# Attention of the first layer in 37 steps of up to four pairs of heads instead of 56 steps of one pair

## The reference

```python
def even_layer(x, mem_n, ...):
    h = rms_norm(x, norm_g)
    (nq, nkc, nvc, nks, nvs, nkw, nvw, ng, nz, mq, mk, mv, mz, eq, ez) = _split(h @ w_in, EVEN_SPLITS)
    gates = sigmoid(ng + gate_b)                       # 3 branches x 8 heads
    a_out = nsa_attention(rot(nq), kc, vc, rot(nks), nvs, rot(nkw), nvw, gates)
    b_out = moba_attention(rot(mq), rot(mk), mv)       # 8 heads of 64
    m_out = memory_attention(eq, mem_n, w_mem_kv)      # 4 heads of 64 over 256 memory rows
    y = concatenate([a_out * silu(nz), b_out * silu(mz), m_out * silu(ez)]) @ w_out
    return x + y
```

## Time and profile before

| | us |
|---|---|
| median of 3 runs | 2300.81 (2300.05 to 2301.47) |
| profiled execution | 2301.48 |
| its span, first to last instruction | 2299.7 |
| TensorE busy in the span | 2222.7 (97%) |
| DVE busy | 666.7 (29%) |
| ACT busy | 502.7 (22%) |
| mean granted clock of TensorE | 0.987 |

### The profile page before, as it was taken

The page is one execution under the profiler, slowest core; times in us unless marked ns, Lnnn a source line. Parts: engine busy times, 40 slices in busy tenths (PEclk is TensorE's granted clock), DMA queues, the critical chain, the costliest instruction groups (busy, mean ns, idle before and its releaser), DMA issues. The chain is left out here.

```text
span 2299.7 us, 19928 instructions
## 1 busy us (share of the span) xinstructions
PE 2222.7 (97%) x8070; PEld 1049.2 (46%) x8070; DVE 666.7 (29%) x1189; ACT 502.7 (22%) x996; POOL 0.2 (0%) x4
## 2 busy tenths in 40 slices
PE   9999999999999999999999999999989989999897
PEld 5444455544444444444444455554445333333333
DVE  3355545412311222411343333331140010100134
ACT  3333334310000324211123334230121000000022
POOL 0000000000000000000000000000000000000000
PEclk9899999999999999999999999999999999999998
DMA  9211112122222111123211121132346999999950
GB/s 230 57 37 37 37 37 74 47 82 74 88 92 76 46 49 54 42 81 80 74 61 50 37 74 37 38 83 73 146 165 258 405 409 409 409 409 409 409 207 37
DMA packets 164602, 317.40 MB, mean 138 GB/s; under 512 B 44800, under 2 KB 74624, under 8 KB 164512
## 3 DMA queue, kind: packets, MB, share of 16 engines
q1 hardware_dynamic: 162480, 314.41, 37.8%
q10 hardware_dynamic: 2032, 1.73, 0.3%
HBM read 314.01 MB, written 2.10 MB: 137 GB/s over the span
## 5 line engine op out<-in xcount | busy, mean ns | idle before, releaser
L417 PE MATMUL bank<-hT,ring 128*128 128x512 f32 (+1 forms) x1632 | 742.5, 605 | 6.8 <-ACT hT L579 4.8
L417 PEld LDWEIGHTS bank<-hT,ring 128*128 128x128 f32 (+1 forms) x1632 | 304.5, 192 | 366.4 <-issue 357.5
L417 PE MATMUL bank<-ring,hT 128*128 128x512 f32 (+2 forms) x576 | 219.6, 539 | 0.0
L2255 PE MATMUL bank<-wide,xg 128*64 128x512 f32 x600 | 179.1, 595 | 9.4 <-DMA wide<-in_w_exp_up 2.8
L417 PEld LDWEIGHTS bank<-ring,hT 128*128 128x128 f32 x576 | 103.1, 190 | 106.3 <-issue 102.7
L2255 PE MATMUL bank<-ring,xg 128*64 128x512 f32 x392 | 132.9, 596 | 4.7 <-DMA ring<-in_w_exp_gate 3.4
L417 PE MATMUL bank<-rz,ring 128*128 128x512 f32 x256 | 111.3, 592 | 0.0
L2255 PEld LDWEIGHTS bank<-wide,xg 128*64 128x64 f32 x600 | 54.7, 137 | 97.1 <-issue 96.1
L2290 PE MATMUL bank<-wide,hidT 128*64 128x512 f32 x304 | 89.3, 595 | 6.4 <-ACT hidT L2346 3.5
L417 PEld LDWEIGHTS bank<-rz,ring 128*128 128x128 f32 x256 | 48.6, 190 | 61.2 <-issue 61.0
L1177 ACT ACTIVATE att_pt<-bank 128x512 f32<-128x512 f32 (+3 forms) x56 | 38.6, 688 | 161.4 <-PE bank L1056 161.3
(11 more groups left out here) (433 smaller groups left out, 2218.6 us busy)
## 6 DMA issues: line engine op xcount, KB each, us to landing
wide<-in_w_exp_gate SPq DMA_DIRECT2D x76, 512.0 KB, 12.5
wide<-in_w_exp_down SPq DMA_DIRECT2D x76, 512.0 KB, 13.7
wide<-in_w_exp_up SPq DMA_DIRECT2D x74, 512.0 KB, 13.3
ring<-in_l_w_in SPq DMA_DIRECT2D x18, 2048.0 KB, 7.8
ring<-in_w_exp_gate SPq DMA_DIRECT2D x52, 512.0 KB, 12.2
ring<-in_w_exp_down SPq DMA_DIRECT2D x52, 512.0 KB, 13.2
ring<-in_w_exp_up SPq DMA_DIRECT2D x46, 512.0 KB, 13.5
ring<-in_w_in SPq DMA_DIRECT2D x10, 2048.0 KB, 7.7
```

What stands on the lines that cost most here:

```text
L417: mm = pe.matmul(self.out(n), *mats[i], start=i == 0, stop=i == len(mats) - 1)
L2255: mm = pe.matmul(bank[2 * which + n][e * 64:(e + 1) * 64, :], xg[p // 2 % 2][:, k, s:s + CAP], block_ap(j)[k % 2][:, n * 512:(n + 1) * 512 ...
```

## The change

The units are made of one, two or four pairs, so that their scores fill 512 columns of a bank: query tile t takes `4 // (t + 1)` pairs at once (four of 128 keys, two of 256, one of 384 or 512), the memory two of 256. NSA's query tiles come in the order 3, 2, 1, 0. That makes 22 units of NSA (8, 8, 4, 2), 11 of MoBA (1, 2, 4, 4) and 4 of memory: 37. The instructions of DVE on a unit span its pairs; the exponentials are still one per head and pair. The dense jobs are cut into four quarters, of two products each (112 in all), and laid evenly over the 37 steps: three in each, four in the last. The four jobs of mz and their block of weights come before those of mv. Silu and the gating of groups move to the steps that follow from this; the small statistics' tile `att_stats` is placed in the arena.

```diff
-            ("mq", 1816, 512), ("mk", 2328, 512), ("mv", 2840, 512), ("mz", 3352, 512)]:
+            ("mq", 1816, 512), ("mk", 2328, 512), ("mz", 3352, 512), ("mv", 2840, 512)]:
...
+        def several(t):
+            n = 4 // (t + 1)
+            return [range(i, i + n) for i in range(0, 4, n)]
+
+        for t in reversed(range(TT)):
+            groups.append(dict(first=len(units), y=proj[:, NZ:NZ + 4, t * P:(t + 1) * P], tile=t))
+            for branch, tile in ((1, NKS), (2, NKW)):
+                keys = [proj[e * 64:(e + 1) * 64, tile, 0:(t + 1) * P] for e in range(2)]
+                share = gates[:, t, 8 * branch:8 * branch + 8].rearrange("p (g i) -> p g i", g=2)
+                for some in several(t):
+                    add_unit([(heads_of(NQ + i, t), keys) for i in some], t + 1,
...
-        def planned(n, parts=2):
-            nonlocal slot_at
+        def planned(n, parts=4):
             step = 8 // parts
             for i in range(parts):
-                plan[slot_at].append((n, i * step, (i + 1) * step))
-                slot_at += 1
+                quarters.append([(n, i * step, (i + 1) * step)])
 
         def planned_turns():
             n = len(jobs)
             flush()
-            for x in range(n, len(jobs)):
-                plan[slot_at - 1].append((x, 0, 8))
+            quarters[-1].extend((x, 0, 8) for x in range(n, len(jobs)))
...
+        z_at = len(jobs)
+        fm_row(EVEN["mz"], 0, MZ)
+        planned(len(jobs) - 1)
+        planned_turns()
...
+        plan = [[x for q in quarters[len(quarters) * s // NU:len(quarters) * (s + 1) // NU] for x in q] for s in range(NU)]
+        plan[0].insert(0, (0, 0, 8))
...
+            silu_at[ends[some[-1]] + 1] = [(n, tile + i) for i, n in enumerate(some)]
...
-                        for e in range(2):
-                            mm = pe.matmul(psum[:, 2 + e, 0:u["w"]], u["q"][e], u["k"][e], start=True, stop=True)
+                        w = u["w"]
+                        for j, (q, k) in enumerate(u["pairs"]):
+                            for e in range(2):
+                                mm = pe.matmul(psum[:, 2 + e, j * w:(j + 1) * w], q[e], k[e], start=True, stop=True)
...
-                        dve.tensor_reduce(nm, psum[:, 2:4, 0:w], AX.X, ALU.max, negate=True).then_inc(a_peak, 1)
+                        dve.tensor_reduce(nm, scores, AX.X, ALU.max, negate=True).then_inc(a_peak, 1)
...
-                        for e in range(2):
-                            ins = act.activation(probs[s % 3][:, e, 0:u["w"]], psum[:, 2 + e, 0:u["w"]], ACT.Exp,
-                                                 bias=nm[:, e:e + 1], accum_out=tot[:, e:e + 1])
+                        for j in range(u["n"]):
+                            for e in range(2):
+                                ins = act.activation(probs[s % 3][:, e, j * w:(j + 1) * w],
+                                                     psum[:, 2 + e, j * w:(j + 1) * w], ACT.Exp,
+                                                     bias=nm[:, e, j:j + 1], accum_out=tot[:, e, j:j + 1])
```

More of the change, by code:

```diff
@@ L911, in heads_of @@
             return [proj[e * 64:(e + 1) * 64, tile, t * P:(t + 1) * P] for e in range(2)]
[L913 to L917, removed]
-        for t in range(TT):
[L920 to L930, removed]
+        def add_unit(pairs, blocks, v, mask, cols, share=None):
+            units.append(dict(pairs=pairs, n=len(pairs), w=P * blocks, v=v, mask=mask, cols=cols, share=share,
+                              group=len(groups) - 1))
+            groups[-1]["last"] = len(units) - 1
@@ new lines, in several @@
+        def several(t):
[8 more added lines that the diff above has]
+                    add_unit([(heads_of(NQ + i, t), keys) for i in some], t + 1,
+                             lambda b, e, j, c=128 * branch - 128: nv[:, b, c + e * 64:c + (e + 1) * 64], t * P,
+                             [i * P for i in some], share[:, :, some[0]:some[-1] + 1])
@@ new lines, in build @@
+        for t in range(TT):
+            groups.append(dict(first=len(units), y=proj[:, MZ:MZ + 4, t * P:(t + 1) * P]))
+            for some in several(t):
+                add_unit([(heads_of(MQ + i, t), [proj[e * 64:(e + 1) * 64, MK + i, 0:(t + 1) * P] for e in range(2)])
+                          for i in some], t + 1,
+                         lambda b, e, j, i0=some[0]: mv[:, b, (2 * (i0 + j) + e) * 64:(2 * (i0 + j) + e + 1) * 64], t * P,
+                         [i * P for i in some])
@@ L931, in build @@
         for half in range(2):
-            group(4, proj[:, EZ:EZ + 2, half * MEM:(half + 1) * MEM])
+            groups.append(dict(first=len(units), y=proj[:, EZ:EZ + 2, half * MEM:(half + 1) * MEM]))
             for t in (2 * half, 2 * half + 1):
[L934 to L937, removed]
+                add_unit([(heads_of(EQ + i, t), [memk[0][e * 64:(e + 1) * 64, i, :] for e in range(2)]) for i in range(2)],
+                         2, lambda b, e, j: memv[0][:, b, (2 * j + e) * 64:(2 * j + e + 1) * 64], None,
+                         [i * MEM + t % 2 * P for i in range(2)])
@@ L969, in build @@
             turn.append((MK + i, n))
+        z_at = len(jobs)
+        fm_row(EVEN["mz"], 0, MZ)
+        planned(len(jobs) - 1)
+        planned_turns()
+        zs = [z_at]
+        for i in range(1, 4):
+            zs.append(len(jobs))
+            fm_row(EVEN["mz"], i * P, MZ + i)
+            planned(zs[-1])
         for t in range(TT):
@@ L1054, in _ @@
                         for e in range(2):
-                            for b in range(units[n]["w"] // P):
+                            for b in range(units[n]["n"] * units[n]["w"] // P):
                                 mm = pe.transpose(psum[:, 4 + e, b * P:(b + 1) * P], probs[n % 3][:, e, b * P:(b + 1) * P],
@@ L1079, in _ @@
                             pe.wait_ge(a_out, g - 1)
[L1080 to L1084 removed]
+                        nb = u["w"] // P
+                        for j, col in enumerate(u["cols"]):
+                            for b in range(nb):
+                                for e in range(2):
+                                    mm = pe.matmul(o[e * 64:(e + 1) * 64, col:col + P], u["v"](b, e, j),
+                                                   turned[n % 2][:, e, (j * nb + b) * P:(j * nb + b + 1) * P],
+                                                   start=n == grp["first"] and j == 0 and b == 0,
+                                                   stop=False, skip_group_check=True)
                         mm.then_inc(a_value, 1)
@@ L1135, in _ @@
                         u = units[s]
-                        w = u["w"]
-                        nm, tot, rv_ = (ast[:, s % 3, x, :] for x in range(3))
+                        nj, w = u["n"], u["w"]
+                        nm, tot, rv_ = (ast[:, s % 3, x, :, 0:nj] for x in range(3))
+                        scores = psum[:, 2:4, 0:nj * w].rearrange("p e (j w) -> p e j w", j=nj)
                         dve.wait_ge(a_score, s + 1)
@@ L1183, in _ @@
                         u = units[s]
-                        nm, tot = (ast[:, s % 3, x, :] for x in range(2))
+                        w = u["w"]
+                        nm, tot = (ast[:, s % 3, x] for x in range(2))
                         act.wait_ge(a_peak, s + 1)
```

51 lines of the change are left out of this document (23 added, 28 removed).

## The result

The changed kernel takes 2288.86 us in the median of 5 runs (2286.21 to 2293.41), against 2300.81 before: the ratio is 0.995 (95% interval 0.9938 to 0.9963), so 12 us less, between 8.5 and 14.3. The profiled execution took 2286.21 us, its span 2284.4.

What follows compares the result with a forecast made beforehand. TensorE's own order of work was taken to bound the stage, with DVE and ACT waits costing nothing. Steps -13.7, rotary's stall +2.5, drain +2.0, clock +2.2 gave -7.0 us: median 2293.8 us, 80% between 2289.5 and 2298.0.

Steps and rivals of the forecast that it cites:

- rotary's stall: Step 17, MK+3's rotary before mz's second product: TensorE waits for DVE to empty the bank, a new stall of 2.5 us.
- clock behind the four rotaries: Behind the four rotaries in a row after mk's first: shorter idles, clock stays at 1.00, no fall counted.
- The clock: Granted clock after TensorE idles: one fall behind the new drain, 2.2 us; none counted behind the rotary's stall.
- Fewer steps: TensorE over the stage: 37 steps rather than 56, each costing 0.72 us beyond its columns, saves 13.7 us.
- Rival 3: Overhead belongs to the pair, not the step, at least in the scores: 3.8 us come back, 2297.6 us; 9%.
- The cover: Four-pair steps: TensorE has 7.4 us of work over a 5.7 us score chain, leaving 1.7 us, so no wait for exponentials.
- The drain: From the last scores to w_out's first product: 11.35 us with an Exp table load, 2.0 us more idle than before.
- Rival 1: No clock falls, or the stalls are hidden: 2291.6 us, or 2289.1 with the rotary's stall hidden too; 20%.
- Rivals 2: The clock falls at both the rotary's stall and the drain, or the drain is longer: 2295.5 to 2297.5 us; 24%.
- rival 4: Slower: TensorE at half speed for 12 us behind each of the rotary's stall and the drain, 2303.6 us; 4%.
- The sign I gave: Forecast is wrong if w_out's first product, at 448.08 us before, doesn't begin between 438 and 441 us.

Runs made afterwards that it cites:

- one pair: The changed kernel's order and machinery, but one pair in each unit, 56 steps of two quarter products: 2297.46 us against 2297.84 before, 0.9995.
- both edits: Changed kernel with MK+3's rotary issued inside mz's first job and the Exp table loaded behind the last Silu: 2285.65 us, 0.9939 of before.

## Why the prediction was wrong, step by step

The stage, by its terms (the stage's means of three profiles each):

| term | predicted | measured | from |
|---|---|---|---|
| 19 steps | -13.7 | -13.1 | one pair against both edits |
| rotary's stall | +2.5 | +2.2 | idle 1.92; the stage is 2.2 shorter without it |
| drain, idle more | +2.0 | +2.0 | 11.36 at full clock, 11.35 predicted |
| clock behind the drain | +2.2 | +1.1 | 2.28, 1.03, 0 |
| clock behind the 64 small products | not counted | -1.7 | the eight in 5.40 against 3.70, in every profile |
| clock behind the four rotaries | counted as 0 | -1.1 | 0, 1.6, 1.6 in before, 0 in after |
| sum | -7.0 | -10.6 | stage means: -10.6 |

That the sum meets the means to 0.1 is better than its terms are known: the first rests on one profile of each kernel, and the two kernels between them divide it into 0.64 and 0.73 a step. The clock at the head of the stage costs both kernels the same in the mean.

**The step that failed is "The clock".** It said that one fall is added behind the drain and counted none taken away. It went through the idles only, and asked of each whether the clock falls. The runs showed in its place: the fall behind the drain is there in 2 of 4 profiles with that idle and costs 1.1 us in the mean of the changed kernel's three, where 2.2 were counted; and the stage of before had a fall of its own in 3 of 3, worth 1.7 us, behind the compressed branch's scores, that the new order of the tiles takes away. The trace of before held it, eight dense instructions in 5.40 us; a read of the granted clock over the whole stage would have shown it, where the earlier trace rows began at 201 us and the earlier trace rows ended at 110. That the clock stayed at 1.00 behind the four rotaries held for the one profile read; it fell there in the two further ones of before, and in none of the eight others that have the same two waits. That term may be chance.

Of the 4.9 us between the time predicted and the median, 3.6 lie in the stage, by the means; the other 1.3 lie outside it, and their cause stays open (below).

**The rotary's stall** was the right mechanism, priced a little too high. Counted from the end of step 16's scores (249.48), TensorE stood ready at 4.45 us, not 4.2, and DVE had emptied the bank at 6.3, not 6.65 (5.87 and 0.69 add up to 6.56).

**Fewer steps** was right: 8.45 us in a four-block step, 0.69 a step from two kernels. **Rival 3** did not come: the scores of a four-pair step start at 285.07, the transposes at 286.16, 1.09 later, for two pairs it is 1.07 (below), for one pair 1.06 (above).

```profile
248.41 1.14 PE L1048 MATMUL bank<-proj 64*128 64x256 f32 x8
249.48 0.87 PE L1065 MATMUL bank<-cst,att_p 128*128 128x128 f32 x6
...
285.07 1.16 PE L1048 MATMUL bank<-proj 64*128 64x128 f32 x16
286.16 1.09 PE L1065 MATMUL bank<-cst,att_p 128*128 128x128 f32 x8
```

**The cover** held. The chain of that four-pair step, DVE's mask and reduce, the first and last of the eight exponentials, the scaling, and TensorE's next scores:

```profile
286.28 1.23 DVE L1156 TENSOR_TENSOR bank<-bank,cst 128x1024 f32<-128x1024 f32 x1 [2.89 <-PE bank L1048]
287.55 1.22 DVE L1160 TENSOR_REDUCE att_stats<-bank 128x8 f32<-128x1024 f32 x1
288.81 0.37 ACT L1209 ACTIVATE att_p<-bank,att_stats 128x128 f32<-128x128 f32 x1 [0.49 <-DVE att_stats L1160]
...
291.23 0.39 ACT L1209 ACTIVATE att_p<-bank,att_stats 128x128 f32<-128x128 f32 x1
292.18 1.22 DVE L1178 TENSOR_TENSOR att_p<-att_p,att_stats 128x1024 f32<-128x1024 f32 x1
293.56 1.16 PE L1048 MATMUL bank<-proj 64*128 64x128 f32 x16
```

Counted from the end of the scores at 286.16, the exponentials end 5.5 us later, at 291.6 (5.7 predicted); the next scores come 1.9 later (1.7). **The drain** was right to 0.01 us at full clock, the table load in it included: it begins at 424.73, the exponential at 426.03, 1.30 later. The drain of some 1.38 us that the Trainium skill, "ScalarE: Activation LUTs", section "What ACT_TABLE_LOAD costs", puts on every switch is not seen here either: taking the whole load out of the chain brought 1.43 us.

**Rival 1** named 2289.1 for "no clock falls, stalls hidden", and the median came to 2288.86; but the stalls were not hidden, so that was luck. Rivals 2 and 4 did not come: behind the rotary's stall the clock never fell, and where it fell behind the drain it was back at 1.00 when w_out's products began, 6.7 us later at most, where rival 4 took 12.

**The sign I gave** for w_out's first product, 438 to 441 us, was missed at 436.20; 3.4 us of that lie ahead of S and are chance, and the second profile of the same kernel, with S at 103.11, has it at 438.36.

**What stays open.** Behind W all kernels agree to 0.02 us until the idle of 2.82 us in the next stage, 833.63 us later. There they part, in the same instructions. As a further mark take the first product with `ffn_acc` behind it: it begins at W + 1242.10 to 1242.87 in the three profiles of before and the one of one pair; of the nine merged ones five have it at W + 1242.25 to 1242.84 and four at 1238.46 to 1239.63. The difference is how much the clock fell behind that idle: by windows of 4 us, what it lacks to 1.00 adds up to 5.1 us in the nine profiles that come late, to 1.7 in three of the early ones, and to nothing in the first profile of the changed kernel. From W to the end it is 1852.0 us in the mean of the first four and 1850.6 in the nine. This would be 1.5 us more of gain (2.4 by the three profiles of after), which with the stage's 10.6 makes the 12 that were timed. Whether the changed kernel shifts these falls or the four came so by chance the profiles don't tell. Nor was it tried which property of the wide first steps (longer dense runs, or what stands between them) keeps the clock up behind the 64 products.

## What to carry to other kernels

A step of small product groups costs TensorE a fixed sum beyond its columns: measure it from two step widths in the trace, and merge units until a bank is full; here 0.72 us a step by the trace stood against 0.69 by the experiments. Before a restructuring, read the granted clock over the whole stretch in windows, in the old kernel too: the change moves the places where the clock falls, and a fall removed counts as much as one added. Where single profiles differ in code that is the same, take three of each kernel and cut them at common marks, or chance is read as cause.

## What the runs showed of the hardware

- The clock fell to its lower level (1.2 GHz; 0.50 of full where a whole window lay in a fall) without any idle of TensorE ahead of it: right behind 3.66 us of 64 products of 32 columns, with narrow steps ahead of them, in three profiles of three. Behind the same products after wide steps it stayed at 1.00 (2.4 GHz), ten of ten.
- The same idle of 2.54 us was followed by a fall in two profiles and by none in two; one of 1.11 us by none in five. One of 2.82 us, in code that is the same, was followed by a fall in twelve profiles of thirteen (windows of 4 us lack 5.1 us of full clock in nine of them, 1.7 in three). In the stage a fall cost 1.0 to 2.3 us. Single times of the same code spread over 8.6 us at 2300; the clock is what differs in the same code of the profiles, and for the runs without a profile that is not shown.
- A switch of group on TensorE (dense, 64-row pairs of scores, transposes, paired values) costs 0.16 to 0.20 us by the two step widths of before; with one, two and four pairs the scores took 1.06, 1.07 and 1.09 us.
